# Fetching the expert weights of a top-2-of-32 mixture layer in two halves of each slot

## The reference, cut to what matters

```python
# hf: 1088 x 1024; per token one of 4 groups, in it the best 2 of 8 experts -> 2 of 32
act = silu(einsum("td,edf->tef", hf, w_gate)) * einsum("td,edf->tef", hf, w_up)   # f = 256
out = einsum("tef,efd->td", act * combine[..., None], w_down)
```

## Time and profile before

| what | value |
|---|---|
| median of 3 runs | 1109.02 us (1104.05 to 1110.41) |
| the profiled execution's own time | 1104.13 us |
| its span on the core | 1102.4 us |
| PE busy | 1052.0 us (95%) |
| DVE / ACT / POOL busy | 702.9 / 289.1 / 184.5 us |
| DMA queue q1 (SP's) | 54336 packets, 168.82 MB |
| DMA queue q0 (POOL's) | 20928 packets, 35.09 MB |

### The profile page before, as it was taken

One profiled execution on the slowest core, in us unless ns is written; L12 is line 12 of the kernel. 1 busy time (PEld: TensorE's weight loads), 2 busy tenths in 40 slices (PEclk: granted clock), 3 DMA queues, 4 the chain that ended last, 5 costly groups with the idle time before them and its releaser, 6 DMA issues.

```text
span 1102.4 us, 15581 instructions
## 1 busy us (share of the span) xinstructions
PE 1052.0 (95%) x6119; PEld 603.1 (55%) x6119; DVE 702.9 (64%) x1389; ACT 289.1 (26%) x587; POOL 184.5 (17%) x229
## 2 busy tenths in 40 slices
PE   6999999999999999999999999989999999998992
PEld 4666766787764444888766645545533333333330
DVE  5576699947858665743376676877754455555446
ACT  5200341568821111100033301110411222222223
POOL 5000200101000000000000000000133445554455
PEclk9999999999999999999999999999999999999997
DMA  9109450297546004100244450015899999999972
GB/s 303 50 1 212 48 43 1 89 281 256 215 170 183 1 1 155 74 1 1 80 187 154 155 227 39 20 58 202 299 285 414 413 414 413 414 415 412 412 261 80
DMA packets 75468, 204.97 MB, mean 186 GB/s; under 512 B 25592, under 2 KB 34448, under 8 KB 67056
## 3 DMA queue, kind: packets, MB, share of 16 engines
q1 hardware_dynamic: 54336, 168.82, 43.4%
q0 software_dynamic: 20928, 35.09, 9.5%
q10 hardware_dynamic: 128, 0.03, 0.0%
HBM read 195.23 MB, written 52.18 MB: 224 GB/s over the span
## 4 chain that ended last, share of the span: by engine, by line
PE 77%; DMA 9%; DVE 5%; issue 3%; ACT 2%; SPq 2%; POOL 1%; ACTq 0%; POOLq 0%; DVEq 0%
PE bank L832 16%; PE bank L1004 9%; PE bank L1304 9%; PE bank L1069 9%; PE bank L1199 6%; DMA arena<-in_w_up 5%; PE bank L1322 4%; PE bank L802 3%; PE bank L963 3%; PE bank L1101 3%; PE bank L1166 3%; DMA arena<-in_w_down 2%; DMA arena<-work_rows,slots_in 2%; PE bank L1248 1%; PE bank L986 1%
## 5 line engine op out<-in xcount | busy, mean ns | idle before, releaser
L832 PE MATMUL bank<-arena 128*128 128x360 f32 (+1 forms) x576 | 177.7, 468 | 0.9 <-DVE arena L1853 0.9
L1304 PE MATMUL bank<-arena 128*32 128x512 f32 x1536 | 170.6, 594 | 6.4 <-DMA arena<-in_w_up 6.4
L832 PEld LDWEIGHTS bank<-arena 128*128 128x128 f32 x576 | 108.5, 190 | 64.7 <-issue 1.4
L2172 DVE TENSOR_TENSOR arena<-arena,bank 128x512 f32<-128x512 f32 (+3 forms) x56 | 68.4, 1221 | 65.0 <-PE bank L1069 37.4
L1304 PEld LDWEIGHTS bank<-arena 128*32 128x32 f32 x1536 | 49.2, 110 | 107.4 <-issue 107.0
L1004 PE MATMUL bank<-arena 128*128 128x272 f32 x448 | 103.0, 392 | 0.0
L1199 PE MATMUL bank<-arena 128*128 128x512 f32 x224 | 100.6, 598 | 2.2 <-DVE arena L2337 2.2
L1069 PE MATMUL bank<-arena 128*128 128x512 f32 x224 | 97.7, 593 | 0.0
L1004 PEld LDWEIGHTS bank<-arena 128*128 128x128 f32 x448 | 85.0, 190 | 17.4
L1322 PE MATMUL bank<-arena 128*32 128x512 f32 x768 | 87.5, 593 | 3.1 <-ACT arena L1726 2.1
L1498 ACT ACTIVATE arena<-bank 128x272 f32<-128x272 f32 (+5 forms) x94 | 41.9, 451 | 170.2 <-PE bank L832 122.1
(11 more groups left out here) (474 smaller groups left out, 1474.5 us busy)
## 6 DMA issues: line engine op xcount, KB each, us to landing
arena<-in_w_gate SPq DMA_DIRECT2D x32, 1024.0 KB
arena<-in_w_up SPq DMA_DIRECT2D x32, 1024.0 KB
arena<-in_w_down SPq DMA_DIRECT2D x32, 1024.0 KB
arena<-in_ck SPq DMA_DIRECT2D x8, 1024.0 KB, 7.1
arena<-in_cv SPq DMA_DIRECT2D x8, 1024.0 KB, 5.4
arena<-in_w_in SPq DMA_DIRECT2D x3, 2048.0 KB, 14.1
work_firsts<-in_x SPq DMA_DIRECT2D x1, 4352.0 KB
arena<-in_x SPq DMA_DIRECT2D x8, 512.0 KB, 6.0
```

The source lines that it names most:

```text
L832: last = nc.tensor.matmul(b[:, 0:w], win[slot][:, k, m * P:m * P + P], ht[:, k, c0:c0 + w], start=k == 0, stop=k == KD - 1)
L1304: last = nc.tensor.matmul(bank[2 + j % 2][t0:t0 + QT, :].rearrange("p (h n) -> p h n", h=2), (xgt[j % 2] if j else xgt_first)[:, k, t0:t0 ...
L2172: V.tensor_tensor(out, out, bank[banks(n)][:, :].unsqueeze(1).to_broadcast([P, width, 512]), ADD).then_inc(sem["md_free"], 1)
```

## The change

The transfers of gate and up weights into a released slot are cut in two along k: rows k = 0 to 3 of each partition and rows k = 4 to 7. PE raises a new semaphore, `gu_half`, when the matmul of k = 3 of a round is issued last of its four quarters and done. SP now waits for `gu_half` of the old expert's last round and issues the first halves of gate and up (2 transfers of 512 KiB, in pieces of 4 KiB), then waits for `gu_full` and issues the second halves. Where a round releases two slots, both first halves go ahead of both second halves. PE still waits for the whole slot before a round, by a count that is 64 a refill in place of 32. The five first fetches and the down weights are as they were.

```diff
+        def in_halves(e):
+            return e >= GUB
+        def gate_fills(e):
+            return sum(64 if in_halves(o) else 32 for o in range(e % GUB, e + 1, GUB))
...
+            def load_gu_half(e, slot, k0):
+                for h, w in enumerate(("w_gate", "w_up")):
+                    sp.dma_start(gu[slot][:, h, k0:k0 + 4, :], weights(w, e, "p k")[:, k0:k0 + 4, :]).then_inc(sem[f"gu_in{slot}"], 16)
...
             for j in range(NR + 1):
+                for k0 in (0, 4):
+                    for e in range(NE - GUB):
+                        if last_round(e) == j and in_halves(e + GUB):
+                            sp.wait_ge(sem["gu_full" if k0 else "gu_half"], j + 1)
+                            load_gu_half(e + GUB, e % GUB, k0)
                 for e in range(NE - GUB):
-                    if last_round(e) == j:
+                    if last_round(e) == j and not in_halves(e + GUB):
                         sp.wait_ge(sem["gu_full"], j + 1)
                         load_gu(e + GUB, e % GUB, sem[f"gu_in{e % GUB}"])
...
             def gate_up(j, k0=0, k1=KD):
                 for e in experts(j):
-                    pe.wait_ge(sem[f"gu_in{e % GUB}"], (e // GUB + 1) * 32)
+                    pe.wait_ge(sem[f"gu_in{e % GUB}"], gate_fills(e))
...
+                    if k == 3:
+                        last.then_inc(sem["gu_half"], 1)
```

More of the change, by code:

```diff
@@ L61 @@
 a_ok r48_ok ctl_ok idx_ok gu_in0 gu_in1 gu_in2 gu_in3 gu_in4 dn_in0 dn_in1 dn_in2 dn_in3 dn_in4
-xg_in0 xg_in1 xg_in2 xg_in3 t_full t_free gu_full silu_ok prod_ok rk_full ix_full dve_x ht_full htm_ok
+xg_in0 xg_in1 xg_in2 xg_in3 t_full t_free gu_half gu_full silu_ok prod_ok rk_full ix_full dve_x ht_full htm_ok
 d_full ya_ok zt_ok y_st0 y_st1 x_go xw_in role_ok wt_ok wt_st yg_in0 yg_in1 yg_in2 yg_in3
```

## The result

| | before | changed |
|---|---|---|
| median of 20 runs | 1108.58 us (1104.05 to 1110.41) | 1111.38 us (1107.68 to 1113.46) |
| ratio | 1 | 1.0026 (95% interval 1.0017 to 1.0035) |
| the profiled execution's span | 1102.4 us | 1110.2 us |

The change makes the kernel slower by 2.8 us, a quarter of a per cent: measurable over 20 runs, and within the half per cent that the prediction calls about what runs of this kernel can tell from no change. 1111.1 us was forecast.

The account below looks back on a forecast made before the run. The prediction took the DMA engines as the bound from the first refills to round 22's start, then a tail of PE. Smaller pieces 3.4 less early issue 1.3 gave +2.1 us: 1109.02 + 2.1 = 1111.1 us, range 1102 to 1118.

Parts of the forecast that it names:

- The bound: DMA engines set the pace from the first refills to round 22's start: 12.2 us of transfers a round against PE's 11.69.
- The signs: 62112 SP packets, DMA full from about 810.7 us, rate up to 2% under 413 GB/s, up-weight waits staying or growing.
- Smaller pieces, +3.4 us: Gate and up refills: 6912 pieces of 8 KiB become 13824 of 4 KiB, costing 3.4 us by rates, ends 1.9 and 5.7.
- 5.7 us from packet times: Upper end for the smaller pieces: two 4 KiB packets take 323 ns against 310 for one of 8 KiB.
- Early issue, -1.3 us: First refill, round 1: starts at 808.1 instead of 810.50, bringing every later transfer 1.3 us forward; later rounds gain nothing.
- upper bound of 2.35: Most the early issue could gain, in us, if the whole earlier start of the first refill counts.
- SP's issues hide in its waits for PE: 54 more issues of 0.34 us on SP cost nothing, covered by its 76.6 us of waiting for PE.
- Order in pairs, more transfers: Refills: second halves behind both first halves cost nothing in the sum; 54 more transfers cost nothing visible, 1.4 us at most.
- The sum: Start of round 22 and all after it: 3.4 - 1.3 = +2.1 us, ends -0.5 and +7.1; chance 0.60.
- The latency rival: Rounds wait because slots are released too late, so halves remove the waits: 1101.3 us, chance 0.10.
- the rival of no effect: 4 KiB pieces run as fast as 8 KiB in the mixed load: 1107.7 to 1109.0 us, chance 0.12.
- The two slower rivals: Dead time per transfer in the full queue, 1116.5 us, chance 0.10; pairs' order in rounds 17 and 20, 1116.1, chance 0.08.

Follow-up runs that it names:

- e4: Kernel before, with the up weights of all experts from the sixth on left out: ratio 0.9886 to the kernel before.
- e1: Kernel before, with only the slot layout changed so that each 1 MiB gate or up transfer goes in 4 KiB pieces: ratio 1.0019.
- e2: Changed kernel without the early issue, both halves waiting for the end of the round: ratio 1.0043 to the kernel before.
- e8: Changed kernel with halves and early issue for experts 5 and 6 only, later refills as before: ratio 0.9999 to the kernel before.
- e10: The changed kernel itself, run again: ratio 1.0027 to the kernel before.
- e6: Changed kernel with pairs in order, the first expert's second half ahead of the second's first half: ratio 1.0047 to the kernel before.
- e3: Kernel before, with the down weights in 8 KiB pieces and PE's transposes reading every second column: ratio 1.0159.

## Why the prediction was right, step by step

*The bound.* Right. The DMA engines stay full, and their rate decides: e4. One reading was a little off: PE is not free of waits up to 950 us, for 830 to 850 us show 19.46 us of 20 (a wait of 0.5 us for down weights).

*The signs.* SP's queue has 62112 packets, as forecast to the last one; the rate fell by 1.7%, within the 2%; the waits for up weights grew. Round 22 came 8.0 us later on the span's clock and 2.9 us later counted from round 0. One sign came only in part, that the DMA would be full from about 810.7 us.

```profile
813.00:814.00 1.00, 1.00 (x12) 0.26 (x8) 0.86 (x2) 0.00 (x0) 0.74 (x1) 1.00 0.89 242
...
817.00:818.00 1.00, 1.00 (x12) 0.30 (x13) 0.00 (x0) 0.00 (x0) 0.00 (x0) 1.00 1.04 263
...
821.00:822.00 1.00, 1.00 (x12) 0.26 (x8) 0.44 (x3) 0.00 (x0) 0.00 (x0) 1.00 1.02 406
```

The engines were busy there, but at 242 to 347 GB/s until 821 us: of the 1672 packets in 811 to 821 us, 984 were under 512 B, against 153 of 615 in the kernel before.

*Smaller pieces, +3.4 us.* Right in mechanism; the size stays open within some 2 to 6 us. The rate gives 4.1 us for the window of 224 us, e1's timing 2.1 (0.7 to 3.5), e2's 4.7 with its late halves (3.0 to 6.5), the profiles of e1 and e2 from round 0 to round 22 6.1 and 6.6. The 3.4 lie among these; the other bound, 5.7 us from packet times, isn't excluded. The quiet transfers of the earlier trace rows foretold the sign of what happened in a full queue. The Trainium skill, "DMA: Bandwidth & Descriptors", section "Why small descriptors are slow (HBM only)", gives by the prediction's estimate 1.2%, some 1.5 us. e1's interval takes that in as well, but the rate stands against it: 1.2% on the gate and up weights, somewhat over half of the bytes, would leave 410 GB/s, and 405 or 406 were measured.

*Early issue, -1.3 us.* Right in sign between e2 and the change, if overlapping intervals may count (0.0017, 1.9 us); not seen in e8. The place was not as forecast. The first refill left at 811.02 and its second half at 815.61:

```profile
811.02 0.34 SPq L499 DMA_DIRECT2D arena<-in_w_gate  x1
...
815.61 0.33 SPq L499 DMA_DIRECT2D arena<-in_w_gate  x1
...
1031.82 1.65 SPq L499 DMA_DIRECT2D arena<-in_w_up  x1
```

The forecast had SP's small issues as what holds the refill up, until 808.1. Here they ended at 809.1, and SP then waited for PE, whose half round ended at 810.96, since PE had lost 5.1 us ahead of round 0. Counted from round 0 the refill left after 23.95 us in place of 28.55: 4.6 us early, twice the upper bound of 2.35. At 44 us after round 0 SP's queue was 1.35 MB ahead of the kernel before (7.55 MB against 6.20 since 14 us after it), which is 3.3 us at 413 GB/s. e10 has the same 4.6 us and 1.36 MB; e6, where PE was 3.3 us late, is 2.3 us early; e8, where it was not late, 1.0 us, and its queue is not ahead (6.11 MB). So the early issue is worth the more, the later PE runs against SP, and the prediction's 2.4 us were worked out for one execution.

*SP's issues hide in its waits for PE.* The cover thinned out, at no cost. SP waited 76.6 us for `gate_up`, and now:

```profile
SPq L499 <- PE bank L1321: 23.9, 12, 3.9
```

It stands in issuing instead: issues longer than 1 us are common from 839 us on in the changed kernel, before from 905. e1, with no more transfers than before, waits 29.1 us, so it is the pieces again: it looks as if the full queue takes fewer bytes ahead when they come in small pieces, which no run tests by itself. It is never empty.

*Order in pairs, more transfers.* Put at nothing. e6 and e2 against e1 leave up to 2 to 3 us open each.

*What I left out.* That the piece size divides the engines between the queues. It worked for the change: PE's waits for rows went from 1.3 us to none. It seems to have cost the sum nothing, since the bytes set the pace. In e3 the same omission made the expectation wrong by 20 us (-2.3 expected, +17.6 measured).

*The sum.* +2.1 forecast; +2.8 measured, +2.9 and +2.1 (e10) from round 0 to round 22. That the sum came this near is in part luck: in the profiles both terms were larger than forecast, 6.1 and 6.6 us for the pieces (e1, e2) and some 3.3 to 4.4 us for the early issue (3.3 by bytes, 3.7 and 4.4 from e2 to the change and to e10), and the errors cancel. The latency rival is out (waits grew), the rival of no effect too (interval from 1.0017). The two slower rivals' sizes, +7.5 and +7.1, are excluded; a smaller price of transfers or order is not.

No run that fetches all the weights was clearly faster than the kernel before. By these runs, what would be so has to take bytes or pieces off the DMA in this stage without making SP's pieces larger than POOL's rows can bear; none of them tried it.

## What to carry to other kernels

When a stage's DMA engines are full, an earlier issue only lengthens the queue, and it can gain only at the stage's start, by as much as the issuing engine stands ready; ask what the edit does to the bytes and to the size of the pieces. A transfer cut in two can halve its contiguous pieces, and here the stage moved 1.7% fewer bytes a second with all weights in 4 KiB pieces than with two thirds of them in 8 KiB. Before making the pieces of one queue larger, look at who shares the engines with it: the gain in rate was 0.7% (413 to 416 GB/s), the loss by rows coming late 1.6% of the whole kernel.

## What the runs showed of the hardware

- A full stage moved 413 GB/s with a third of the weight bytes in 4 KiB pieces, 409 with two thirds, 405 or 406 with all, at a share of 16 engines that stayed full.
- Two queues share the DMA engines as if by pieces: gathers of rows landed in 8.8 us at the median beside 4 KiB pieces (at most 10.0) and in 13.0 beside 8 KiB, up to 20.4.
- With the gate and up weights sent to 64 partitions at a time the stage ran at 221 GB/s, with 128 at 413.
- The same matmuls after the same wait of 2.18 us ran 3.67 us in one execution and 5.37 in another, whose granted clock was lower. The times of single runs scatter by 6 us, and the mean granted clock of the span mostly goes with it: 0.992 for the fastest and 0.988 for the slowest of one and the same kernel.
